# A two-way recurrent scan on one core: the second direction runs half an iteration behind the first

## The reference, cut to what matters

```
xs = (tm(r, r), tm(w_f, w_b), tm(k_f, k_b), tm(v, v), tm(-kk, -kk), tm(kk * a_f, kk * a_b))

def step(st, inp):
    r_t, w_t, k_t, v_t, a_t, b_t = inp
    sa = jnp.einsum('dbhij,dbhj->dbhi', st, a_t)
    st = st * w_t[..., None, :] + sa[..., None] * b_t[..., None, :] + v_t[..., None] * k_t[..., None, :]
    y = jnp.einsum('dbhij,dbhj->dbhi', st, r_t)
    return st, y

_, ys = lax.scan(step, s0, xs)
y = ys[:, 0] + ys[::-1, 1]
```

## Time and profile before

| what | value |
|---|---|
| median of 3 runs | 4511.88 us (4508.41 to 4512.11) |
| the profiled execution, its time | 4510.41 us |
| the profiled execution, its span | 4508.6 us |
| PE busy | 4051.0 us, 90% of the span |
| DVE busy | 2463.5 us, 55% |
| ACT busy | 1757.5 us, 39% |

### The profile page before, as it was taken

How to read it: one execution, slowest core, us unless ns; L and a number is a source line. 1 busy time by engine, 2 the same in 40 slices (tenths; PEclk the granted TensorE clock), 3 DMA queues, 4 the chain that set the end, 5 groups by cost and what they waited for, 6 DMA issues and landing times. The chain is left out here.

```text
span 4508.6 us, 87963 instructions
## 1 busy us (share of the span) xinstructions
PE 4051.0 (90%) x36546; PEld 3942.0 (87%) x36546; DVE 2463.5 (55%) x3376; ACT 1757.5 (39%) x2206; POOL 0.2 (0%) x4
## 2 busy tenths in 40 slices
PE   7999998989988899786899999999898778897898
PEld 7999988989888899676899999999898777796798
DVE  4789765955435544345545545454547554554354
ACT  3434444343443343233344434443344222344443
POOL 0000000000000000000000000000000000000000
PEclk9999999999999998898999999999999888998999
DMA  4555444335444453323454555555544000243343
GB/s 173 170 171 181 146 157 153 113 131 169 148 151 139 156 182 130 128 84 131 142 186 159 184 179 186 178 185 177 169 159 149 3 3 3 86 151 122 131 168 131
DMA packets 99233, 638.34 MB, mean 142 GB/s; under 512 B 11136, under 2 KB 14592, under 8 KB 28224
## 3 DMA queue, kind: packets, MB, share of 16 engines
q1 hardware_dynamic: 98976, 634.65, 41.8%
HBM read 626.18 MB, written 8.42 MB: 141 GB/s over the span
## 5 line engine op out<-in xcount | busy, mean ns | idle before, releaser
L245 PE MATMUL ps_gemm<-arena_r,w_hi 128*128 128x256 f32 (+1 forms) x17088 | 2307.0, 288 | 135.8 <-ACT w_hi L186 46.8
L245 PEld LDWEIGHTS ps_gemm<-arena_r,w_hi 128*128 128x128 f32 (+1 forms) x17088 | 2184.5, 195 | 157.8 <-issue 94.0
L192 DVE TENSOR_TENSOR ring_r<-ring,w_hi 128x1024 fp32r<-128x1024 f32 (+3 forms) x1264 | 1417.8, 1126 | 1326.6 <-ACT w_hi L186 1306.7
L186 ACT ACTIVATE w_hi<-ring 128x1024 fp32r<-128x1024 f32 (+3 forms) x1264 | 1231.3, 979 | 1420.9 <-PE ps_gemm L245 1165.6
L245 PE MATMUL ps_gemm<-arena_r,ring_r 128*128 128x256 f32 (+1 forms) x8544 | 1240.2, 287 | 61.4 <-DVE ring_r L192 60.6
L245 PEld LDWEIGHTS ps_gemm<-arena_r,ring_r 128*128 128x128 f32 (+1 forms) x8544 | 1127.3, 194 | 70.6 <-DVE ring_r L192 68.2
L242 PE MATMUL ps_gemm<-w_hi,arena_r 128*128 128x256 f32 (+1 forms) x1408 | 193.2, 288 | 1.0 <-ACT w_hi L186 0.9
L1008 DVE SCALAR_TENSOR_TENSOR arena<-arena,vecs (+15 forms) x480 | 192.2, 463 | 0.0
L242 PEld LDWEIGHTS ps_gemm<-w_hi,arena_r 128*128 128x128 f32 x1408 | 182.8, 198 | 2.8 <-ACT w_hi L186 1.8
L393 ACT ACTIVATE arena<-ps_gemm 128x512 f32 (+2 forms) x103 | 61.5, 597 | 259.2 <-PE ps_gemm L245 202.1
L1489 PE MATMUL ps_gemm<-arena 64*64 64x64 f32 x2176 | 90.8, 238 | 47.7 <-DVE arena L1608 11.6
(11 more groups left out here) (287 smaller groups left out, 2153.0 us busy)
## 6 DMA issues: line engine op xcount, KB each, us to landing
ring<-in_ff SPq DMA_DIRECT2D x128, 1024.0 KB, 5.0
ring<-in_w_out SPq DMA_DIRECT2D x48, 1024.0 KB, 5.0
ring<-in_gate SPq DMA_DIRECT2D x32, 1024.0 KB, 5.1
ring<-in_conv_a SPq DMA_DIRECT2D x16, 1024.0 KB, 5.1
ring<-in_conv_b SPq DMA_DIRECT2D x16, 1024.0 KB, 5.1
ring<-in_gla_v SPq DMA_DIRECT2D x16, 1024.0 KB, 5.1
ring<-in_conv_z SPq DMA_DIRECT2D x16, 1024.0 KB, 5.0
ring<-in_conv_out SPq DMA_DIRECT2D x16, 1024.0 KB, 5.0
```

The source lines that it names most:

```text
L186: nc.scalar.activation(w_hi[q % 2][:, 0:size], ring[slot][:, part], ACT.Copy).then_inc(hi_ready, 1)
L192: nc.vector.tensor_tensor(ring_lo[slot][:, part], ring[slot][:, part], w_hi[q % 2][:, 0:size].bitcast(F32), ALU.subtract).then_inc(lo_read ...
L245: mm = nc.tensor.matmul(bank[0:cw, 0:T], w[:, k * cols + c * cw:k * cols + (c + 1) * cw], r[:, kk, :], start=start, stop=stop)
```

## The change

`STEPS` gets a twentieth entry, `("y", 0, 1)`, and a generator `turns` replaces the double loop on all three engines. It runs over positions p; at each, direction 0 does its step p and direction 1 its step p - `LAG`, where `LAG` is 10, half of the steps. There are 8 x 20 + 10 = 170 positions: in the first 10 only direction 0 has a step, in the last 10 only direction 1. The semaphores of the preparation become one per direction.

Direction 1 now transposes the values for itself (`q.VT`), so its `tok` has 32 transposes as well. `outputs` goes: in the new step `y` each direction forms its own outputs in its own bank `X`; DVE copies direction 0's into `LW` and later adds direction 1's. ACT's copy of the outputs goes.

`B[0]` is made by one instruction for all 128 partitions instead of two of 64; for that `small` holds the identity of each half. All preparation pieces stand behind the same steps in both directions: `exponents` behind `d4`, `keys` behind `b8`, `operands` behind `tt`; the exponentials behind `d8`. Before the first group, `keys` of both directions now comes ahead of `operands` of either.

```diff
                 q.bkp = tmp2[d][:, :, :]
-                q.tok = carve(early, 256 * (4 - d)).rearrange("p (k c n) -> p k c n", k=4 - d, c=NCH)
+                q.tok = carve(early, 1024).rearrange("p (k c n) -> p k c n", k=4, c=NCH)
+                q.VT = q.tok[:, 3]
                 q.EX = carve(early, 1024).rearrange("p (k n) -> p k n", k=4) if d else stat
...
                 dirs.append(q)
-            VT = dirs[0].tok[:, 3]
-            prep_in, prep_exp, chain, y_done, y_copied, started = stage_sems("exponents", "exponentials", "dve_chain", "y_done", "y_copied", "states_zero")
+            chain, started = stage_sems("dve_chain", "states_zero")
+            prep_in = stage_sems("exponents0", "exponents1")
+            prep_exp = stage_sems("exponentials0", "exponentials1")
             prepared = stage_sems("prepared0", "prepared1")
...
                     STEPS.append((("s", k), 0, 1))
+            STEPS.append(("y", 0, 1))
             NS = len(STEPS)
+            LAG = NS // 2
             NA = sum(x[1] for x in STEPS)
...
 
+            def turns():
+
+                for p in range(NC8 * NS + LAG):
+                    for d, q in enumerate(dirs):
+                        if 0 <= p - d * LAG < NC8 * NS:
+                            it, n = divmod(p - d * LAG, NS)
+                            yield it, n, d, q, STEPS[n][0]
+
             def channels(buf, c):
...
                     v = by(channels(VD, it))
-                    for k, src in enumerate((AR[:, :, 0, :], by(q.bkp[:, 0, :]), by(q.bkp[:, 1, :]), v)[0:4 - d]):
+                    for k, src in enumerate((AR[:, :, 0, :], by(q.bkp[:, 0, :]), by(q.bkp[:, 1, :]), v)):
                         for c in range(NCH):
...
                     each(q.Z, E2, q.B[1])
-                    x = each(q.Y, q.M2[:, :, 0, :], VT)
+                    x = each(q.Y, q.M2[:, :, 0, :], q.VT)
                 elif name == "tt":
...
                     for R in HALVES:
-                        x = mm(q.Z[R, 0:CH], q.tok[R, 2, c, :], VT[R, c, :], start=False, stop=True)
-                return x
-
...
+                elif name == "y":
+                    for c in range(NCH):
                         k = q.order.index(c)
-                        for n, (left, right) in enumerate(((VT[:, c, :], q.M2[:, c, 1, :]), (q.U[:, c, :], q.M1[:, c, 1, :]),
-                                                           (q.S[:, k, :], q.AR[it % 2][:, c, 1, :]))):
+                        for n, (left, right) in enumerate(((q.VT[:, c, :], q.M2[:, c, 1, :]), (q.U[:, c, :], q.M1[:, c, 1, :]), (q.S[:, k, :], AR[:, c, 1, :]))):
                             for R in HALVES:
-                                x = nc.tensor.matmul(y[R, c * CH:(c + 1) * CH], left[R, :], right[R, :], start=d == 0 and n == 0, stop=d == 1 and n == 2)
+                                x = mm(q.X[R, c * CH:(c + 1) * CH], left[R, :], right[R, :], start=n == 0, stop=n == 2)
                 return x
...
                 if name == "tok":
-                    return cp(q.tok, q.XY[:, 0:256 * (4 - d)].rearrange("p (k c n) -> p k c n", k=4 - d, c=NCH))
+                    return cp(q.tok, q.XY[:, :].rearrange("p (k c n) -> p k c n", k=4, c=NCH))
                 if name in ("d2", "n1", "d4"):
...
                     tt(q.RT, q.M1[:, :, 0, :], q.SQ0[:, 1], ALU.subtract)
-                    for R in HALVES:
-                        x = tt(q.B[0][R], q.SQ0[R, 1], ident[R, R].rearrange("p (a n) -> p a n", a=1).broadcast_to([CH, NCH, CH]), ALU.add)
-                    return x
+                    return tt(q.B[0], q.SQ0[:, 1], per_chunk(small[:, :]), ALU.add)
                 if name == "d4":
...
                     return tt(q.TT, Z, q.B[0], ALU.add)
+                if name == "y":
+                    y = channels(LW, it)
+                    if d == 0:
+                        return nc.vector.tensor_copy(y, q.X[:, 0:T])
+                    return tt(y, q.X[:, 0:T], y, ALU.add)
                 c = q.order[name[1]]
...
                     link(dve, v.tensor_copy(incl, q.ka))
-                v.tensor_copy(q.GC[it % 2][:, :], by(q.ka)[:, :, CH - 1]).then_inc(prep_in, 1)
+                v.tensor_copy(q.GC[it % 2][:, :], by(q.ka)[:, :, CH - 1]).then_inc(prep_in[d], 1)
 
...
                 q = dirs[d]
-                act.wait_ge(prep_in, 2 * it + d + 1)
-                nc.scalar.activation(q.EX[:, 3, :], q.EX[:, 0, :], ACT.Exp, scale=-1.0).then_inc(prep_exp, 1)
-                act.wait_ge(prep_exp, it * 6 + 3 * d + 1)
-                nc.scalar.activation(q.EX[:, 0:3, :], q.EX[:, 0:3, :], ACT.Exp).then_inc(prep_exp, 1)
-                nc.scalar.activation(q.GC[it % 2][:, :], q.GC[it % 2][:, :], ACT.Exp).then_inc(prep_exp, 1)
+                act.wait_ge(prep_in[d], it + 1)
+                nc.scalar.activation(q.EX[:, 3, :], q.EX[:, 0, :], ACT.Exp, scale=-1.0).then_inc(prep_exp[d], 1)
+                act.wait_ge(prep_exp[d], it * 3 + 1)
+                nc.scalar.activation(q.EX[:, 0:3, :], q.EX[:, 0:3, :], ACT.Exp).then_inc(prep_exp[d], 1)
+                nc.scalar.activation(q.GC[it % 2][:, :], q.GC[it % 2][:, :], ACT.Exp).then_inc(prep_exp[d], 1)
 
...
                 aa = channels(AA, 8 * d + it)
+                dve.wait_ge(prep_in[d], it + 1)
                 link(dve, v.tensor_tensor(q.ka, channels(VD, 8 + it), aa, ALU.mult))
...
                 AR = q.AR[it % 2]
-                dve.wait_ge(prep_exp, it * 6 + 3 * d + 3)
+                dve.wait_ge(prep_exp[d], it * 3 + 3)
                 v.scalar_tensor_tensor(out=AR[:, :, 0, :], in0=by(channels(VD, 8 + it)), scalar=-1.0, in1=by(q.EX[:, 1, :]), op0=ALU.mult, op1=ALU.mult)
...
                 def _(pe):
-                    pe.wait_ge(started, 1)
-                    for it in range(NC8):
-                        for n, (name, _, _) in enumerate(STEPS):
-                            for d, q in enumerate(dirs):
-                                if n == 0:
-                                    pe.wait_ge(prepared[d], it + 1)
-                                    if it and d == 0:
-                                        pe.wait_ge(y_copied, it)
-                                if it or seen(n, 1):
-                                    pe.wait_ge(act_step[d], it * NA + seen(n, 1))
-                                if it or seen(n, 2):
-                                    pe.wait_ge(dve_step[d], it * ND + seen(n, 2))
-                                pe_emit(it, q, d, name).then_inc(pe_step[d], 1)
-                        for d in range(2):
-                            pe.wait_ge(dve_step[d], it * ND + ND)
-                        outputs(it).then_inc(y_done, 1)
+                    pe.wait_ge(started, 2)
+                    for it, n, d, q, name in turns():
+                        if n == 0:
+                            pe.wait_ge(prepared[d], it + 1)
+                        if it or seen(n, 1):
+                            pe.wait_ge(act_step[d], it * NA + seen(n, 1))
+                        if it or seen(n, 2):
+                            pe.wait_ge(dve_step[d], it * ND + seen(n, 2))
+                        pe_emit(it, q, d, name).then_inc(pe_step[d], 1)
 
...
                         exponentials(act, 0, d)
-                    for it in range(NC8):
-                        for n, (name, a, _) in enumerate(STEPS):
-                            if a:
-                                for d, q in enumerate(dirs):
-                                    act.wait_ge(pe_step[d], it * NS + n + 1)
-                                    act_emit(q, d, name).then_inc(act_step[d], 1)
-                            if name == "t16" and it + 1 < NC8:
-                                exponentials(act, it + 1, 0)
-                            if name == "n2" and it + 1 < NC8:
-                                exponentials(act, it + 1, 1)
-                        act.wait_ge(y_done, it + 1)
-                        nc.scalar.activation(channels(LW, it), dirs[0].X[:, 0:T], ACT.Copy).then_inc(y_copied, 1)
+                    for it, n, d, q, name in turns():
+                        if STEPS[n][1]:
+                            act.wait_ge(pe_step[d], it * NS + n + 1)
+                            act_emit(q, d, name).then_inc(act_step[d], 1)
+                        if name == "d8" and it + 1 < NC8:
+                            exponentials(act, it + 1, d)
 
...
                 def _(dve):
-                    for d, q in enumerate(dirs):
-                        x = nc.vector.memset(q.S[:, 0, :], 0.0)
-                    nc.vector.memset(small[:, :], 0.0).then_inc(started, 1)
-                    dve.wait_ge(started, 1)
+                    for q in dirs:
+                        nc.vector.memset(q.S[:, 0, :], 0.0)
+                    for R in HALVES:
+                        x = nc.vector.tensor_copy(small[R, :], ident[R, R])
+                        x.then_inc(started, 1)
+                    dve.wait_ge(started, 2)
                     for d in range(2):
```

(26 more changed lines are left out.)

7 lines of the change are left out of this document (2 added, 5 removed).

## The result

The changed kernel takes 4549.51 us (median of 4 runs, 4544.26 to 4552.52); the kernel before takes 4510.15 in the runs beside it. The ratio is 1.0088, 95% interval 1.0071 to 1.0106: **slower by 39 us**. The profiled execution took 4549.92 us with a span of 4548.1, 39.5 us longer than before's. The scan lasts from 3490.76 to 3906.65 us, 415.9 us against 374.6: 41.3 us more, and all else is the same to 2 us.

What follows compares the result with a forecast made beforehand. No engine is full: PE's issue and uncovered evacuations bound the scan. Halves of 23.7 us plus 2.4 for the clock, with the ends, sum to 426.8 against 374.6, +52.2 us: median 4564, range 4524 to 4590.

Steps and rivals of the forecast that it cites:

- Evacuation exposed by the pairing: Scan positions: each costs the largest of large issue plus its evacuation, or both issues; the small partner covers 0.12 or 0.24 us.
- The bare half: Half an iteration, ten positions, without preparation or clock loss: 22.2 us.
- the handover from `y` to the next `tok`: Direction 1's next `tok` held back by DVE's work on `y`: about 0.3 us every second half, 0.15 on average.
- Preparation: On DVE: exponents make `d8` 0.95 us late, keys hold `n1` about 0.55, operands cost nothing; together 1.5 us a half.
- The clock: PE in the scan: low clock takes 2.4 us a half, bounds 0 and 4; a loss of 1 to 4 has chance 0.73.
- PE's share of work: PE's full-clock work per iteration is 62% of its length, where it was 68%, so no higher clock is expected.
- The sum: Whole scan: 1.3 + 14 x (23.7 + 2.4) + 2 x (22.2 + 2.4) + 10.9 = 426.8 us, against 374.6: +52.2.
- Ends: First product 1.3 us later by one `keys`; direction 1 alone for its last ten steps, 10.9 us.
- The instruction for `B[0]`: Behind `gram`: one instruction saves half of 0.84 us, 0.42; at worst it saves nothing.
- The page's rule: Scan: by the skill's rule, interleaving latency-bound `u`/`s` with PE-bound steps would bring the stage down to PE's issue time.

Runs made afterwards that it cites:

- lag-0 run: The changed kernel with LAG = 0 and a wait of DVE on its own copy ahead of direction 1's `y`: 4487.4 us, ratio 0.9949 to the kernel before.
- lag-1 order: The changed kernel with LAG = 1, so a large step stands beside another large one: 4480.6 us, ratio 0.9936 to the kernel before.

## Why the prediction was right, and where it was off

The sign, the mechanism and the range were right: +52 forecast, +39 measured, 4549.5 against 4564. At the full clock the path of an iteration grew by 3.8 us; by the prediction's terms it should have grown by 47.4 - 42.8 = 4.6.

- **Evacuation exposed by the pairing.** Shown by the lag-0 run (62 us, of which the path is 4.8 us an iteration and the clock 2.2) and by the timeline. From step to step the full-clock half gives 3.62, 4.70, 1.84, 2.31 us for `tok`, `gram`, `d2`, `d4` and 1.82, 1.17, 2.38 for `n1`, `n2`, `cz`; the prediction had 3.69, 4.68, 1.85, 2.33, 1.85, 1.16, 2.36. The bare half is 22.1 us, 22.2 forecast. The two halves are not alike, as it took them to be: the handover from `y` to the next `tok` took 0.78 us with `tt`'s issue in it, where I had 0.3 in every second half, and the second half has no such handover.
- **Preparation.** 1.5 us a half forecast, 1.2 measured: 2.48 - 1.77 = 0.7 for the exponents in the first half and 0.8 in the second (0.95 forecast), 1.63 - 1.16 = 0.5 for the keys in both (0.55).
- **The clock.** I took 2.4 us a half, that is, nearly the 5.0 us of extra issue time that the low stretches before had. The low stretches of the iteration shown hold 56 + 158 = 214 passes, as many as the 212 before, and the same 5.0 us of extra issue; it is 51.08 - 46.74 = 4.3 us longer than at the full clock. Over five iterations the cost is 4.1 us, 2.05 a half. Both here and in the kernel before (4.8 of 5.0) most of the extra issue lies on the path. That the clock would be no higher I took from PE's share of work at the full clock (62% for 68%), and the granted clock is 0.87 for 0.86; but no run shows that this share decides it.
- **The sum.** From its first product to its last the forecast scan is 426.8 - 1.3 = 425.5 us, the measured one 415.9. The 14 halves with preparation took 357.0 us (3490.76 to 3847.76) for 365.4, of which 4.6 are the half (23.4 for 23.7) and the rest the clock; the last two took 46.2 for 49.2, mainly because the low clock cost 1.2 us there and not 4.8.
- **Ends.** The drain took 12.7 us for 10.9. From the first exponents to the first product took 9.35 us (3481.41 to 3490.76) for 7.77 (3482.58 to 3490.35): 1.6 for 1.3; but the exponents themselves began 1.2 us earlier, so that the first product is only 0.4 us later. What follows the scan is 2 us shorter. Neither was forecast.
- **The instruction for `B[0]`.** I took 0.42 us at its own duration. At lag 10 that is what the 4.70 of `gram` shows. In the kernel before, alone, it was worth 21 us, 1.0 us of path an iteration and the rest the clock. The comparison of the change with the kernel before so hides two moves: +62 from the lag, -23 from the rest.
- **The page's rule.** Interleaving the latency-bound steps with the PE-bound ones did not bring the stage towards PE's issue time: at the full clock PE is busy 17.4 of 24.03 us here, 72%, and 34.0 of 41.90 at lag 0, 81%. The Trainium skill ("Perfetto Trace Analysis", Optimization Strategy) says that performance may be improved by interleaving regimes whose most-contended engines differ. Here it was lost by it, 62 us against lag 0: the partner has to be long enough to cover the other's wait.

What stays open: why the lag-1 order takes no longer than lag 0, and what makes the clock fall in one iteration and not in the next with the same steps.

## What to carry to other kernels

When two independent chains share an in-order engine, pair steps by the length of the wait that each has to cover: a large step beside a large one covers it, a small one beside it leaves it open, and the small steps that were saved are fewer than the waits opened. Cost a change of order as a list of positions, each the largest of "own issue + own evacuation" and "both issues"; this gave the steps of the full-clock half within 0.1 us, apart from what DVE's preparation added, and the bare iteration within 0.4 us at lag 10 and at lag 0, but 1.9 too long at lag 1. To price the clock, take each step where it ran at the full clock in the same kernel; extra products in the waits can delay steps themselves, by 1.5 us an iteration with lag 10 and by nothing in the kernel before. Before a helper is put behind a step of an in-order engine, look which operand of the next step stands behind it.

## What was not expected of the hardware

An edit worth 1.0 us of path an iteration shortened the iteration by 3.3 us, since the clock fell less often: two of five iterations run wholly at 2.4 GHz, where the kernel before has three stretches at 1.2 GHz in each. A wait of 1.65 us in front of `w` was followed by 1.2 GHz in the kernel before and by 2.4 GHz in the edited one. And products that compute nothing, in the waits of the kernel before, made it 33 us faster.
